# Two convolution projection chunks as one block of seven products, its third upper sum on VectorE, and three tap accumulators

## The reference

```python
z = h @ w_in                                  # 2048 x (3*2048 + 2*1024 + 2*2048)
q, k, v, u, ga, gc = jnp.split(z, ...)        # u: 2048 columns, a and g of the convolution
...
a, g = jnp.split(u, 2, axis=-1)               # conformer_conv
h = a * jax.nn.sigmoid(g)
h = lax.conv_general_dilated(h, w_dw, ..., feature_group_count=CONV_WIDTH) + b_dw   # 31 taps, causal
h = jax.nn.silu(layer_norm(h, ln_g, ln_b))
return h @ w_pw2
...
merged = jax.nn.sigmoid(ga) * y_attn + jax.nn.sigmoid(gc) * y_conv
return merged @ w_out
```

## Time and profile before

| what | value |
|---|---|
| median of 3 runs | 2113.19 us |
| lowest to highest of 3 runs | 2112.93 to 2113.49 us |
| profiled execution, first to last instruction (span) | 2109.5 us |
| TensorE busy | 2095.7 us, 99% of the span |
| VectorE busy | 1877.2 us, 89% |
| ScalarE busy | 1402.9 us |
| chain that ended last, by engine | PE 88%, DVE 8%, DMA 2%, ACT 1% |

### The profile page before, as it was taken

How to read it: one execution, slowest core, us unless ns; L and a number is a source line. 1 busy time by engine, 2 the same in 40 slices (tenths; PEclk the granted TensorE clock), 3 DMA queues, 4 the chain that set the end, 5 groups by cost and what they waited for, 6 DMA issues and landing times.

```text
span 2109.5 us, 23778 instructions
## 1 busy us (share of the span) xinstructions
PE 2095.7 (99%) x9386; PEld 1734.6 (82%) x9386; DVE 1877.2 (89%) x1420; ACT 1402.9 (67%) x1313; POOL 216.7 (10%) x345
## 2 busy tenths in 40 slices
PE   9999999999999999999999999999999999999998
PEld 7888888888888888888888888888888888888886
DVE  7899999999996889999999986659899999999996
ACT  6677777777775546766676445335677777777773
POOL 0111111101110001011100000000111111100110
PEclk9999999999999999999999999999999999999999
DMA  9798988888985759998898556755788988899892
GB/s 369 253 295 260 279 270 266 291 300 277 289 279 231 276 158 311 299 269 270 304 301 262 212 185 240 260 178 200 244 294 255 282 272 267 290 302 278 288 285 113
DMA packets 92397, 556.65 MB, mean 264 GB/s; under 512 B 13056, under 2 KB 13440, under 8 KB 35200
## 3 DMA queue, kind: packets, MB, share of 16 engines
q1 hardware_dynamic: 68544, 437.69, 54.7%
q0 software_dynamic: 23744, 117.46, 25.8%
HBM read 534.13 MB, written 20.97 MB: 263 GB/s over the span
## 4 chain that ended last, share of the span: by engine, by line
PE 88%; DVE 8%; DMA 2%; ACT 1%; issue 1%; SPq 0%; DVEq 0%; ACTq 0%
PE acc L2259 14%; PE acc L2261 14%; PE acc L2260 14%; PE tb L2259 12%; PE tb L2261 12%; PE tb L2260 12%; PE acc L2197 3%; PE acc L2199 3%; PE acc L2198 3%; DVE g_lo L1338 3%; DVE cacc L1777 3%; DMA g_raw<-in_groups 1%; PE tb L2245 1%; DVE w_lo L1315 1%; DVE g_raw L1346 1%
## 5 line engine op out<-in xcount | busy, mean ns | idle before, releaser
L1338 DVE TENSOR_TENSOR g_lo<-g_raw,g_hi 128x2048 fp32r<-128x2048 f32 x506 | 1147.6, 2286 | 120.4 <-ACT g_hi L817 119.8
L817 ACT ACTIVATE g_hi<-g_raw 128x2048 fp32r<-128x2048 f32 x506 | 964.4, 1916 | 319.8 <-DVE g_raw L1346 121.5
L2259 PE MATMUL acc<-g_hi,xF_hi 128*128 128x512 f32 x1184 | 464.3, 392 | 0.6 <-ACT acc L899 0.6
L2261 PE MATMUL acc<-g_hi,xF_lo 128*128 128x512 f32 x1184 | 461.1, 389 | 0.0
L2260 PE MATMUL acc<-g_lo,xF_hi 128*128 128x512 f32 x1184 | 460.7, 389 | 0.0
L2259 PE MATMUL tb<-g_hi,xF_hi 128*128 128x512 f32 x760 | 296.3, 390 | 0.3 <-DVE g_lo L1338 0.2
L2261 PE MATMUL tb<-g_hi,xF_lo 128*128 128x512 f32 x760 | 295.7, 389 | 0.0
L2260 PE MATMUL tb<-g_lo,xF_hi 128*128 128x512 f32 x760 | 295.7, 389 | 0.0
L1346 DVE TENSOR_TENSOR g_raw<-g_raw,g_raw 128x2048 f32<-128x2048 f32 x120 | 274.3, 2286 | 1.3
L2259 PEld LDWEIGHTS acc<-g_hi,xF_hi 128*128 128x128 f32 x1184 | 222.3, 188 | 46.8 <-ACT acc L899 1.0
L2261 PEld LDWEIGHTS acc<-g_hi,xF_lo 128*128 128x128 f32 x1184 | 222.2, 188 | 46.8
(11 more groups left out here) (180 smaller groups left out, 2307.7 us busy)
## 6 DMA issues: line engine op xcount, KB each, us to landing
g_raw<-in_groups SPq DMA_DIRECT2D x356, 1024.0 KB, 7.2
g_raw<-in_groups POOLq DMA_DIRECT2D x80, 1024.0 KB, 8.6
raw<-in_stream SPq DMA_DIRECT2D x80, 512.0 KB, 4.5
bounce<-h_sq POOLq DMA_DIRECT2D x40, 256.0 KB, 5.5
h_in<-bounce POOLq DMA_DIRECT2D x160, 64.0 KB, 2.6
ln_gb<-in_ln SPq DMA_DIRECT2D x6, 1024.0 KB, 6.6
g_raw<-in_groups SPq DMA_DIRECT2D x6, 512.0 KB, 9.7
res<-in_x_rows SPq DMA_DIRECT2D x1, 2048.0 KB, 16.6
```

What stands on the lines that cost most here:

```text
L817: act.activation(g_hi[:, n % RING], source[:], ACT.Copy).then_inc(g_hi_ready, 1)
L1338: dve.tensor_tensor(g_lo[:, n % RING], source[:], f32(g_hi[:, n % RING]), ALU.subtract).then_inc(g_lo_ready, 1)
L2259: pe.matmul(bank, x_hi_ap, g_hi[:, n % RING, blk], start=begin, stop=False, skip_group_check=True)
L2261: return pe.matmul(bank, x_lo_ap, g_hi[:, n % RING, blk], start=False, stop=end, skip_group_check=True)
```

## The change

The two plain chunks gate 1 and value 1 (8 groups, 192 matmuls) become one seven-product block `CONV` = -1 without a query chunk (14 groups, 168 matmuls). Of its upper sums VectorE makes T1a, T1b, T2a, T3a and T2b; T3b, T4a and T4b are transfers. In the other blocks T1b is a transfer or, beside heads, VectorE's. The gate is emptied from X and Y by the sigmoid into `k_sb` at the start of block 0 on ScalarE, the value by the block's `values` into `vt`, and their product is made in block 0 behind the `g_lo` of Q1; `turn_conv(1)` moves behind Q1 on TensorE. The 33 taps behind the convolution chunks go; each block gets 3 more, the gate groups 9 and 7 for 8 and 6, `attn_out` as before 3 behind each unit, and the rest (9 for 2) at the same place in its third chunk. The taps run in rounds of 2, 3 and 3 tiles with a third accumulator `cacc_last`. The core of the diff, the new programs of the engines (ScalarE, VectorE, GpSimd, TensorE) among it:

```diff
-HEAD_TAPS = (0, 0, 0, 0, 2, 2, 3, 3, 3, 3)
-BLOCK_TAPS = ((3, 3, 1, 1, 3, 1, 1, 1, 1, 1), *([HEAD_TAPS] * NG), (1, 1, 2, 2, 1, 2, 2, 2, 2, 2))
+HEAD_TAPS = (0, 0, 0, 0, 3, 3, 3, 3, 3, 4)
+BLOCK_TAPS = ((3, 3, 2, 2, 3, 1, 1, 2, 1, 1), *([HEAD_TAPS] * NG), (1, 1, 3, 3, 2, 2, 2, 2, 2, 2))
+TAP_ROUNDS = ((0, 1), (2, 3, 4), (5, 6, 7))
...
+            def conv_pair():
+
+                f, g = "mix", CONV
+                split_loaded(f, g, "P1a", "qa")
+                split_loaded(f, g, "P1b", "qb")
+                split_sum(f, g, "P5a", "qa", "T1a")
+                split_sum(f, g, "P5b", "qb", "T1b")
+                fork(f, g, acc[:, BY], acc[:, BX], "P1b")
+                split_sum(f, g, "P6a", "qa", "T2a")
+                split_loaded(f, g, "P3a", "ua")
+                split_sum(f, g, "P6b", "qb", "T2b")
+                act.wait_ge(acc_out[1], 2)
+                fork(f, g, acc[:, BZ], acc[:, BW], "P5b")
+                split_loaded(f, g, "P3b", "ub")
+                conv_block(0)
+                split_sum(f, g, "P7a", "ra", "T3a")
+                act.wait_ge(t3b_ready, fulls(f, g))
+                split(f, g, "P7b", "rb")
+                save_value(g, 0, "P6b")
+                split_loaded(f, g, "P2a", "ga")
+                act.wait_ge(t4a_ready, fulls(f, g))
+                split(f, g, "P4a", "qa")
+                act.wait_ge(t4b_ready, 16)
+                split(f, g, "P4b", "qb")
+                save_value(g, 1, "P7b")
+                split_loaded(f, g, "P2b", "gb")
+
+            def conv_gate_out(t):
+
+                act.wait_ge(g_used, mix_used(CONV, ("P2b", "P4b")[t]))
+                act.activation(k_sb[:, t], acc[:, (BY, BX)[t]], ACT.Sigmoid).then_inc(k_out, 1)
...
+                if not g:
+                    conv_gate_out(1)
                 split_loaded(f, g, "P1a", "qa")
                 if g:
                     keys_out(g - 1, 0)
+                else:
+                    conv_gate_out(0)
                 split_loaded(f, g, "P1b", "qb")
...
-            for g in range(8, 15):
-                split_conv(g)
-            conv_block(0)
-            split_conv(15)
-            conv_gate(1)
+            conv_pair()
...
+            def tap(m):
+
+                for n, tiles in enumerate(TAP_ROUNDS):
+                    if m < TAPS * len(tiles):
+                        j, k = m // len(tiles), m % len(tiles)
+                        return j, k, tiles[k], len(tiles if j or not n else TAP_ROUNDS[n - 1])
+                    m -= TAPS * len(tiles)
+
             def taps(count):
 
                 for m in range(taps_done[0], min(taps_done[0] + count, KC * TAPS)):
-                    pair, n = m // (2 * TAPS), m % (2 * TAPS)
-                    k, j = n % 2, n // 2
-                    c = 2 * pair + k
-                    if n == 0:
-                        dve.wait_ge(ch_ready, 2 if pair < 2 else 4)
+                    j, k, c, behind = tap(m)
+                    if j == 0 and k == 0:
+                        dve.wait_ge(ch_ready, 2 if c == 0 else 4)
                     rows = ch[:, c, j:j + T]
                     w = cw[:, c * TAPS + j:c * TAPS + j + 1]
-                    dve.wait_ge(conv_step, m + 1)
+                    dve.wait_ge(conv_step, max(2, m + 3 - behind))
                     if j == 0:
...
+            def conv_pair():
+
+                f, g = "mix", CONV
+                qa, qb, ra, rb, ua, ub = (source(f, g, name) for name in ("qa", "qb", "ra", "rb", "ua", "ub"))
+                lo_group(f, g, "P1a", "qa")
+                load_done(f, g, "ra")
+                split_done(f, g, "P1a")
+                add(qa, qa, ra)
+                lo_group(f, g, "P1b", "qb")
+                load_done(f, g, "rb")
+                split_done(f, g, "P1b")
+                add(qb, qb, rb)
+                lo_group(f, g, "P5a", "qa")
+                load_done(f, g, "ua")
+                split_done(f, g, "P5a")
+                add(qa, qa, ua)
+                conv_value(0)
+                add(ra, ra, ua)
+                lo_group(f, g, "P5b", "qb")
+                load_done(f, g, "ub")
+                split_done(f, g, "P5b")
+                add(qb, qb, ub)
+                lo_group(f, g, "P6a", "qa")
+                lo_group(f, g, "P3a", "ua")
+                lo_group(f, g, "P6b", "qb")
+                lo_group(f, g, "P3b", "ub")
+                lo_group(f, g, "P7a", "ra")
+                lo_group(f, g, "P7b", "rb")
+                lo_group(f, g, "P2a", "ga")
+                lo_group(f, g, "P4a", "qa")
+                lo_group(f, g, "P4b", "qb")
+                lo_group(f, g, "P2b", "gb")
+                values(g)
+
+            def conv_pair_value():
+
+                dve.wait_ge(k_out, TT)
+                dve.wait_ge(v_out, TT)
+                for t in range(TT):
+                    dve.tensor_tensor(act_sb[:, t], k_sb[:, t], vt[:, t], ALU.mult).then_inc(acc_out[1], 1)
...
-            lo_conv(8)
-            lo_conv(9)
-            lo_conv(10)
-            conv_value(0)
-            lo_conv(11)
-            lo_conv(12)
-            lo_conv(13)
+            conv_pair()
             dve.wait_ge(cw_loaded, 32)
             dve.wait_ge(kept_out, 16 * TT * ND)
-            taps(11)
-            lo_conv(14)
-            taps(11)
-            lo_conv(15)
-            taps(11)
             dve.wait_ge(alibi_loaded, 16)
...
-                taps(6 if g - 1 in HEADS_AT else 8)
+                taps(7 if g - 1 in HEADS_AT else 9)
...
+            def conv_pair_sums():
+
+                f, g = "mix", CONV
+                pool.wait_ge(t_ready, G.sum_no[f, g, "T1b"])
+                add_from_hbm(f, g, "rb", "ub", t3b_ready)
+                pool.wait_ge(g_lo_ready, lo_count(G.at[f, g, "P6a"]))
+                add_from_hbm(f, g, "qa", "ga", t4a_ready)
+                pool.wait_ge(g_lo_ready, lo_count(G.at[f, g, "P6b"]))
+                add_from_hbm(f, g, "qb", "gb", t4b_ready)
...
+            def conv_pair():
+
+                f, g = "mix", CONV
+                X, Y, Z, W = (acc[:, bank] for bank in (BX, BY, BZ, BW))
+                pe.wait_ge(acc_out[0], 2)
+                product_group(f, g, "P1a", X, A11, 0, begin=True)
+                product_group(f, g, "P1b", X, A11, 1)
+                pe.wait_ge(x_lo, 11 + 4 * factors("mix"))
+                pe.wait_ge(acc_out[1], 2)
+                product_group(f, g, "P5a", W, S1, 0, begin=True)
+                product_group(f, g, "P5b", W, S1, 1)
+                turn_conv(0)
+                wait_fork(f, g, 0)
+                product_group(f, g, "P6a", X, S2, 0)
+                wait_fork(f, g, 1)
+                product_group(f, g, "P3a", Z, S4, 0)
+                product_group(f, g, "P6b", X, S2, 1)
+                product_group(f, g, "P3b", Z, S4, 1)
+                wait_fork(f, g, 2)
+                product_group(f, g, "P7a", X, S3, 0)
+                product_group(f, g, "P7b", X, S3, 1)
+                product_group(f, g, "P2a", Y, A12, 0)
+                wait_fork(f, g, 3)
+                product_group(f, g, "P4a", X, A22, 0)
+                product_group(f, g, "P4b", X, A22, 1)
+                product_group(f, g, "P2b", Y, A12, 1)
+
...
-                if g:
-                    pe.wait_ge(k_out, 2 * g)
-                else:
-                    pe.wait_ge(acc_out[0], 4)
+                pe.wait_ge(k_out, evicted(g - 1) if g else 1)
                 product_group(f, g, "P1a", X, A11, 0, begin=True)
                 product_group(f, g, "P1b", X, A11, 1)
                 if g:
                     pe.wait_ge(q_out, 2 * g)
-                else:
+                query_group(g, 0)
+                if not g:
                     turn_conv(1)
-                query_group(g, 0)
                 query_group(g, 1)
-                if g:
-                    pe.wait_ge(v_out, 2 * g)
-                else:
-                    pe.wait_ge(acc_out[1], 4)
```

69 lines of the change are left out of this document (42 added, 27 removed).

## The result

The changed kernel takes 2125.0 us (median of four runs, 2120.6 to 2126.0) where the kernel before takes 2113.1: ratio 1.0054, interval 1.0040 to 1.0068. Measured again beside the experiments it was 2126.3 (five runs, 2121.4 to 2127.8) against 2112.3, ratio 1.0059 (1.0046 to 1.0071). Slower, as forecast, but by 12 to 14 us and not by 7.3: the first median lies 0.5 us inside the upper end of the range (2116.0 to 2125.5), the second 0.8 us outside. The profiled execution took 2124.9 with a span of 2123.0, 13.5 more than before.

The account below looks back on a forecast made before the run. TensorE, busy 99% of the span, bounds the kernel, with VectorE at 89% feeding it; 2.0 + 1.9 + 3.4 = 7.3 us takes the median from 2113.19 to 2120.5, range 2116.0 to 2125.5.

Parts of the forecast that it names:

- Part 1: TensorE's matmuls: 192 become 168, saving 5.4 us if TensorE never waits more than before.
- Part 2: New block and block 0's start: VectorE's line and splits behind sigmoids cost 7.4, with the matmuls saved +2.0 us.
- What I cost at nothing: New block: accumulating transfers for P4a and P4b have 15 and 13 us of cover, so no loss.
- (c): Rival: transfers become the bound in the new block and block 2, 5 to 8 us above forecast, 2126 to 2128; chance 0.08.
- my 2.20: Price in us of each long VectorE instruction, g_lo or sum, taken from the starts of neighbouring g_lo.
- Part 3: Heads, blocks 1 to 4: three more taps each send keys and queries 1.2 us later; scores lose +1.9 us.
- The queries' copy ends at 915.16 + 1.15: Blocks 2 to 4: copy's end against scores' start leaves slack of none, 0.4 and 1.3 us.
- Part 4: Gate groups and `attn_out`: extra taps delay the last g_lo and unit splits; TensorE loses 2.5 and 0.9, +3.4 us.
- (b): Rival: block costs its 2.0 us but the taps' lateness is taken up, 2115.2 to 2117.4 us; chance 0.14.
- (a): Rival: the block is covered and the 5.4 us saved come through, 2107.8 us, faster by 0.26%; chance 0.06.
- (d): Rival: clock falls to half rate at three new waits above 1.5 us, 2.3 us each, 2127.4 us; chance 0.04.
- The three signs: Would refute if seen: block 0's P3a before 794, scores waiting at most 1 us, `attn_out` starting without a `w_lo` wait.

Follow-up runs that it names:

- e1: Kernel before with only the change's tap table: 33 taps moved from the convolution chunks to blocks 0 to 5 and gate groups; 2115.2 us, ratio 1.0017.
- e5: Changed kernel with taps put where VectorE waits: eight ahead of P4a's g_lo, five behind T2b in blocks 1 to 4; 2119.5 us, ratio 1.0034.
- e3: Changed kernel with ScalarE's two splits of block 0 (P1a, P1b) ahead of the two sigmoids; 2119.5 us, ratio 1.0038.
- e7: Changed kernel with taps where VectorE waits, block 0's splits ahead of the sigmoids, and T3a by a transfer; 2110.9 us, ratio 0.9995.
- e12: Changed kernel with two tap accumulators as before instead of three; 2124.9 us, ratio 1.0056.
- e9: e7 with ScalarE's copy to Z ahead of the split of P6b in block 0; 2112.7 us, ratio 1.0001.
- e10: Changed kernel again, nothing altered, for a second time and trace; 2126.3 us, ratio 1.0059.

## Why the prediction was right in sign and short in size

The sum was 7.3 us and the kernel took 12.0 and 14.0 more. Every part has the right sign and place, and that the first median lies inside the range, by 0.5 us, is luck.

**Part 1** held: 24 matmuls fewer, 5.4 us.

**Part 2 (+2.0) came out at +4.0**, of which 0.4 had come ahead of it (4.5 in the second trace, from the same start). The chain was as told, and its waits fell where they were forecast: P5a, P5b, P6a, P1a (2.35 for 2.3), Q1 (1.15 for 1.6), P3a. P4a was not forecast, and two things were missing. First, "What I cost at nothing: the two accumulating transfers". The transfer for T4b was started at 743.70, and P4b's split, which waits for it, could start only at 756.73. The rows of the change, GpSimd's start of the transfer, and on ScalarE this split and the copy behind it:

```profile
743.70 0.86 POOL L2190 DMA_DIRECT2D g_raw<-in_groups  x1 [3.44 <-DVE g_lo L1390]
```

```profile
756.73 1.92 ACT L840 ACTIVATE g_hi<-g_raw 128x2048 fp32r<-128x2048 f32 x1 [4.40 <-DMA g_raw<-in_groups]
758.55 0.57 ACT L922 ACTIVATE act_sb<-acc 128x512 f32<-128x512 f32 x1
```

These 13.0 us (12.7 to 14.9 in the ten traces with the block) are far above the median of 9.3 in the earlier trace rows. P4b, which had 13 us of cover, was still in time. P4a was not: it adds to bank X, which this copy has to read first, and ScalarE's program has the copy behind P4b's split. So P4a hung on T4b, and not on T4a, which had landed by 750.41. The forecast gave P4a its own transfer's 15 us of slack and left this order out. P4a lost 1.0 us with its restart in the first trace and 1.9 in the second: rival (c) in small, by a path that it doesn't name. No run puts the copy ahead of the split. Second, in the first trace P6a was 1.2 later than worked out: VectorE began 0.4 late, and a sum that waits for its own `g_lo` starts 2.38 behind it (714.93, 717.31) and not 2.20, four times ahead of P6a:

```profile
714.93 2.28 DVE L1390 TENSOR_TENSOR g_lo<-g_raw,g_hi 128x2048 fp32r<-128x2048 f32 x1
717.31 2.29 DVE L1398 TENSOR_TENSOR g_raw<-g_raw,g_raw 128x2048 f32<-128x2048 f32 x1
```

Here the page that I had weighed against the row, the Trainium skill, "VectorE: DVE Perf Modes", section "The DRAIN you can't avoid", is nearer to the measurement than my 2.20: where the next instruction needs the output of the one before, it does start behind its end. Where it doesn't (eight `g_lo` in a row, 17.94 us, 2.24 each), the row is nearer, and the section says too that a next op that isn't held starts earlier.

**Part 3 (+1.9) came out at +5.2 (6.0 in the second trace), and this is the step that failed.** The taps' share was right: TensorE is ready for the scores of blocks 2 to 4 15.1, 15.6 and 15.4 us behind the transposes where it was 16.4 to 16.7 before, 1 us less, as three taps say, and e1 with its taps alone lost 1.2. What failed is "The queries' copy ends at 915.16 + 1.15" and the slacks of none, 0.4 and 1.3 read from it: I took the landing of a transfer in one execution of the kernel before as fixed. It scatters by 1 to 2 us a block, and with the new block it comes 0.7 us later in the mean, 1.4 in block 4; before, the slack ate most of that, and now each late landing is a wait: 0.66, 2.82, 0.66 and 1.07 against a single 0.79. In block 1, for which I had forecast nothing, there is no tap's lateness at all, just a landing 1.9 us later than in my one trace. The 3.3 us by which the stretch exceeds the forecast are these landings by the rows. The runs show that they go with the block (1.0 to 4.6 lost without more taps there, 0.5 and 0.6 without the block); no experiment shows what in the block moves them.

**Part 4 (+3.4) held:** +4.3 and +3.5 in the two traces, +3.8 with the taps alone, 0.0 with the taps elsewhere. The three units lose 2.8 us (0.56, 0.66, 0.68 and a restart each; forecast 2.5), the longer wait for `sig_a` 1.0 (forecast 0.9); 0.6 came ahead of `attn_out`.

**Rivals.** (b), the lateness taken up, is refuted by e1 and e5. (a) needed block 0's splits ahead of the sigmoids; with that order (e3), and without the other losses (e7), the block reaches the time of the kernel before and not 5.4 us less. (c), transfers as the bound, came in part: P4a's 1.0 to 1.9 and the landings of part 3 are over half of what the sum fell short by. (d), the clock, was set down as a price of 2.3 us, three times; it comes in some executions, in one place or two, and cost about 1 us in the trace above and 2 in e12. The Trainium skill, "TensorE: Matmul & The Clock Gate", section "HAM oscillation — how this bites in real kernels", which I had set beside it, is borne out in that waits of this kernel are followed by half rate; that every wait is, the traces do not show.

**The three signs** named ahead of the result: P3a of block 0 not before 794 (798.26), the scores waiting over 1 us in all (5.2), a wait for `w_lo` at the start of `attn_out` (1.9). All three came.

## What to carry to other kernels

Work moved off one stretch of a nearly full engine is paid for wherever that engine has no gap: the 33 taps cost about 5 us in unbroken stretches (e1; 2.8 net, since they left another), and with 28 taps put in front of instructions that wait the loss in `attn_out` was gone (e5), so look up the idle time ahead of each instruction before choosing a place. Where two engines meet behind a transfer, take its time from several executions and cost the slack against the longest, not the one that a single trace shows, and look which other instruction stands behind the one that waits (P4b's split, and the copy for which P4a waited). And a wait's releaser is the last of several: before moving it, look what else the waiting instruction needs and when that was ready (e9: 0.2 us earlier, so nothing gained).

## What was unexpected

Three small losses added when repaired together: 5.5, 5.5 and 3.0 alone, 14.1 for all three. That this agrees to 0.1 is chance: against the kernel before beside each they are 4.9, 4.7 and 2.4 alone and 13.2 together, and with e10 as the change 6.9, 6.7 and 4.4 and 15.3. The granted clock fell to its lower level behind a wait of 2.35 us in one trace of six, behind score waits of 2.39, 3.38 and 3.57 in three, and not behind one of 2.82. And P4a, its own operands ready, lost 1.0 and 1.9 us to a copy that stood behind another group's transfer.
